# The modulation column loads of a two-block network move from SyncE's DMA queue to GpSimd's

## What is computed

```
# block 1
mod = silu(c) @ w_ada + b_ada                    # shift, scale, gate: 3 x 2048
h   = rms_norm(x) * (1 + scale) + shift
z   = h @ w_in                                   # u, v, g, q, k, v, g, f (f has 16 columns)
y   = concat(spatial gating, forgetting attention) @ w_out
x   = x + gate * y
# block 2: layer 0 (context + gated linear attention + conv), layer 1 (pooling mixer)
mod_i = silu(c_2) @ w_ada_2[i] + b_ada_2[i]      # 3 x 2048 for each of two layers
modc  = silu(c_ctx_2) @ w_ada_2[0]               # shift and scale of the 256 context tokens
x   = layer_norm(alpha * x + gate_i * mixer_i(x * (1 + scale_i) + shift_i))
```

## Time and profile before

| | |
|---|---|
| runs, median of 3 | 3305.11 us (3304.21 to 3306.54) |
| span of the profiled execution | 3300.8 us |
| its own time, taken as the median | 3305.11 us, so 4.3 us lie around the span |
| PE busy (matmul) | 2958.6 us, 90% |
| PE weight load | 2348.7 us, 71% |
| DVE busy | 1836.1 us, 56% |
| ACT busy | 1066.8 us, 32% |
| POOL busy | 3.9 us, 10 instructions |
| DMA | 451.54 MB, mean 137 GB/s, 41.4% of 16 engines |
| PE in the chain that ended last | 80% |
| mean granted TensorE clock | 0.942 |

### The profile page before, as it was taken

The page is one execution under the profiler, slowest core; times in us unless marked ns, Lnnn a source line. Parts: engine busy times, 40 slices in busy tenths (PEclk is TensorE's granted clock), DMA queues, the critical chain, the costliest instruction groups (busy, mean ns, idle before and its releaser), DMA issues.

```text
span 3300.8 us, 39727 instructions
## 1 busy us (share of the span) xinstructions
PE 2958.6 (90%) x13275; PEld 2348.7 (71%) x13275; DVE 1836.1 (56%) x2889; ACT 1066.8 (32%) x1714; POOL 3.9 (0%) x10
## 2 busy tenths in 40 slices
PE   3499999989999969599999999999899698999996
PEld 2377887666777847378878687787788477787784
DVE  6857763444577454355437456473866666324443
ACT  2332222333332254322233435342322421223324
POOL 0000000000000000000000000000000000000000
PEclk8699999999999979799999999999999799999997
DMA  9766552222356436165522222224566263332331
GB/s 370 272 197 189 185 165 68 64 64 64 108 166 208 166 101 216 62 216 191 167 83 77 70 65 94 70 76 138 181 204 205 75 218 121 91 100 89 111 114 51
DMA packets 219344, 451.54 MB, mean 137 GB/s; under 512 B 23752, under 2 KB 29338, under 8 KB 214860
## 3 DMA queue, kind: packets, MB, share of 16 engines
q1 hardware_dynamic: 219212, 449.82, 41.4%
HBM read 422.47 MB, written 27.30 MB: 136 GB/s over the span
## 4 chain that ended last, share of the span: by engine, by line
PE 80%; DVE 6%; ACT 4%; issue 3%; DVEq 2%; DMA 2%; ACTq 1%; SPq 1%; PEldq 0%; PEld 0%
PE ps L1006 19%; PE ps L1008 19%; PE ps L1007 19%; PE ps L1015 3%; PE ps L1016 3%; PE ps L1017 3%; PE ps L1348 3%; PE ps L985 1%; PE ps L1058 1%; PE ps L1213 1%; PE ps L1221 1%; DMA a_raw<-in_w_ada 1%; DVE acc L1593 1%; PE ps L1381 1%; PE ps L1378 1%
## 5 line engine op out<-in xcount | busy, mean ns | idle before, releaser
L1006 PE MATMUL ps<-op_hi,w_hi 128*128 128x512 f32 (+2 forms) x2928 | 1186.0, 405 | 105.8 <-DVE op_lo L1505 47.3
L1008 PE MATMUL ps<-op_hi,w_lo 128*128 128x512 f32 (+2 forms) x2928 | 1158.4, 396 | 0.0
L1007 PE MATMUL ps<-op_lo,w_hi 128*128 128x512 f32 (+2 forms) x2928 | 1158.0, 396 | 0.0
L1006 PEld LDWEIGHTS ps<-op_hi,w_hi 128*128 128x128 f32 (+1 forms) x2928 | 562.9, 192 | 251.5 <-issue 58.3
L1457 DVE TENSOR_TENSOR w_lo<-w_raw,w_hi 128x512 fp32r<-128x512 f32 x496 | 342.3, 692 | 596.9 <-ACT w_hi L570 592.2
L1008 PEld LDWEIGHTS ps<-op_hi,w_lo 128*128 128x128 f32 (+1 forms) x2928 | 561.8, 192 | 122.5
L1007 PEld LDWEIGHTS ps<-op_lo,w_hi 128*128 128x128 f32 (+1 forms) x2928 | 563.8, 193 | 112.8 <-issue 1.7
L570 ACT ACTIVATE w_hi<-w_raw 128x512 fp32r<-128x512 f32 x496 | 313.0, 632 | 1022.1 <-PE ps L1008 849.1
L1419 DVE SCALAR_TENSOR_TENSOR acc<-a_raw,vec,acc 128x512 f32<-128x512 f32 x576 | 419.7, 747 | 22.5 <-DMA a_raw<-in_w_ada 22.0
L1405 DVE TENSOR_TENSOR w_lo<-w_raw,w_hi 128x512 fp32r<-128x512 f32 (+2 forms) x240 | 145.6, 610 | 207.7 <-ACT w_hi L546 206.8
L546 ACT ACTIVATE w_hi<-w_raw 128x512 fp32r<-128x512 f32 (+2 forms) x240 | 134.8, 565 | 366.8 <-PE ps L1008 285.6
(11 more groups left out here) (208 smaller groups left out, 2245.0 us busy)
## 6 DMA issues: line engine op xcount, KB each, us to landing
a_raw<-in_w_ada SPq DMA_DIRECT2D x224, 512.0 KB, 4.0
w_raw<-in_w_in_e SPq DMA_DIRECT2D x160, 512.0 KB, 4.3
w_raw<-in_w_in SPq DMA_DIRECT2D x112, 512.0 KB, 4.8
arena<-in_w_ada SPq DMA_DIRECT2D x64, 512.0 KB, 8.0
w_raw<-in_w_in_o SPq DMA_DIRECT2D x64, 512.0 KB, 4.2
w_raw<-in_w_out SPq DMA_DIRECT2D x32, 512.0 KB, 5.0
w_raw<-in_w_out_e SPq DMA_DIRECT2D x32, 512.0 KB, 5.0
w_raw<-in_w_out_o SPq DMA_DIRECT2D x32, 512.0 KB, 3.6
```

The lines of the kernel that those rows point to most:

```text
L1006: mm(dst, hi[:, cols], B.op_hi[:, k, 0:tok], start=first, stop=False)
L1007: mm(dst, hi[:, cols], B.op_lo[:, k, 0:tok], start=False, stop=False)
L1008: last = mm(dst, lo[:, cols], B.op_hi[:, k, 0:tok], start=False, stop=last_t)
```

## The change

The 224 loads of `a_raw` are taken out of SP's program and written into GpSimd's (`part_loads`), each with the wait that it had. SP's groups with a part become the same two-turn loop as the others. GpSimd's six memsets stand between the loads in program order.

```diff
-    def modulation(n, m):
-        part, o = GROUPS[n]["part"], ordinal(n)
-        if part is None:
-            return
-        ...
-        if o or m >= 2:
-            sp.wait_ge(sem("part_tile"), KT * o + 2 * m - 2)
-        sp.dma_start(B.a_raw[:, m % 2, :, :], src[:, 2 * m:2 * m + 2, c:c + GC]).then_inc(B.a_in[m % 2], 16)
-
     def stream(n, middle=None):
         pairs = GROUPS[n]["kt"] // 2
-        before = n and GROUPS[n - 1]["part"] is not None
-        if GROUPS[n]["part"] is None and not before and not middle and pairs == 8 and GROUPS[n]["name"] != "egb":
+        if n and not middle and pairs == 8 and GROUPS[n]["name"] != "egb":
             with sp.Fori(0, 2) as r:
                 for m in range(4):
                     weights(n, m, r)
@@
-            if m < LAG and before and not (middle and m == 2):
-                modulation(n - 1, 8 - LAG + m)
             if middle and m == 1:
-                if before:
-                    modulation(n - 1, 7)
                 middle()
-            if m >= LAG:
-                modulation(n, m - LAG)
@@
+def part_loads(B, pool, groups):
+    for n in groups:
+        part, o = GROUPS[n]["part"], ordinal(n)
+        if part is None:
+            continue
+        src = B.A["w_ada"][0] if part < 12 else B.A["w_ada_2"][(part - 12) // 12]
+        src = src.rearrange("(k p) n -> p k n", p=P)
+        c = part % 12 * GC
+        for m in range(KT // 2):
+            if o or m >= 2:
+                pool.wait_ge(B.sem("part_tile"), KT * o + 2 * m - 2)
+            B.nc.gpsimd.dma_start(B.a_raw[:, m % 2, :, :], src[:, 2 * m:2 * m + 2, c:c + GC]).then_inc(B.a_in[m % 2], 16)
+
 def pool_program(B, pool):
     nc, sem, at = B.nc, B.sem, B.at
     n = FIRST["wo1"]
+    pool.wait_ge(sem("masks_made"), 1)
+    part_loads(B, pool, range(FIRST["wo1"] + 1))
 
     pool.wait_ge(B.bank_free[n % 2], n // 2 + 1)
     nc.gpsimd.memset(at(AT_WGC, 1, 2048)[0:33, 0, :], 0.0)
@@
+    part_loads(B, pool, range(FIRST["wo1"] + 1, FIRST["r"]))
     pool.wait_ge(sem("states_out"), 1)
     nc.gpsimd.memset(at(AT_WG, 1, 512)[0:33, 0, :], 0.0)
@@
+    part_loads(B, pool, range(FIRST["r"], FIRST["beside"]))
+    pool.wait_ge(sem("beside_stored"), 16 * (2 * GLA_HEADS + 1))
+    part_loads(B, pool, range(FIRST["beside"], len(GROUPS)))
```

More of the change, by code:

```diff
@@ L300, in weights @@
                      B.weight(g)[:, tiles, g["col"]:g["col"] + g["width"]]).then_inc(B.w_in[slot], 16)
-    def modulation(n, m):
-        part, o = GROUPS[n]["part"], ordinal(n)
-        if part is None:
-            return
-        src = A["w_ada"][0] if part < 12 else A["w_ada_2"][(part - 12) // 12]
-        src = src.rearrange("(k p) n -> p k n", p=P)
-        c = part % 12 * GC
-        if o or m >= 2:
-            sp.wait_ge(sem("part_tile"), KT * o + 2 * m - 2)
-        sp.dma_start(B.a_raw[:, m % 2, :, :], src[:, 2 * m:2 * m + 2, c:c + GC]).then_inc(B.a_in[m % 2], 16)
     def stream(n, middle=None):
         pairs = GROUPS[n]["kt"] // 2
-        before = n and GROUPS[n - 1]["part"] is not None
-        if GROUPS[n]["part"] is None and not before and not middle and pairs == 8 and GROUPS[n]["name"] != "egb":
+        if n and not middle and pairs == 8 and GROUPS[n]["name"] != "egb":
             with sp.Fori(0, 2) as r:
```

## The result

The changed kernel takes 3325.43 us (median of 4 runs, 3323.34 to 3326.93) against 3304.66 us (3302.37 to 3306.54) of the kernel before on the same chip: ratio 1.0062, 95% interval 1.0048 to 1.0076. It is slower by 20.8 us. The prediction was slower, 3318.5 us, range 3306 to 3337.

A forecast was written before the change was run, and what follows sets the result against it. PE was taken to bound most of the chain, with late column loads setting DVE's pace in narrow groups. Terms 6.0 + 5.1 + 1.2 + 1.1 = 13.4 us raised the median 3305.1 to 3318.5 us, range 3306 to 3337.

The forecast's parts named there:

- The bound: PE makes 80% of the chain; it also passes through eight column loads, whose two-buffer loop holds DVE in narrow groups.
- e: Extra time from buffer free to column load landed when GpSimd issues it: 1.4 us, bounded between 0 and 4.
- "f": Group with four column loads on the chain, each later by 1.5 us: 6.0 us lost.
- "ck": Group with three column loads on the chain, each later by 1.7 us: 5.1 us lost.
- "r": Group where each two pairs go over their slack by 0.3 us, four times: 1.2 us lost; first load counted 0.
- "wo1" (1): Group whose first load now stands behind GpSimd's memsets, so PE gets a tile late: 1.1 us lost.
- The other groups: Groups with 12 matmuls a tile: about 7.4 us from release to next reader against 5.4 needed, so nothing added.
- SP's gain: SP is freed of 224 issues of 0.37 us and 1099.5 us of standing, hidden behind the weights' lead: 0.
- The signs: If right: DVE's a_raw wait 35 to 50 us, "f" pieces some 5.7 us, ACT's w_raw wait below 10 us.
- B: Rival: the new queue is nearly as quick as SP, e below 0.7; 3309.3 us at 0.4; chance 0.25.
- C: Rival: faster, column loads on their own ring land in 3.6 us; 3296.7 us; chance 0.09.
- D: Rival: DVE slowed while GpSimd writes its lists, 14 us more in "r"; 3333 us; chance 0.06.

The follow-up runs named there:

- single_by_sync: The kernel before, all loads by SP, with a_raw as four buffers of one k-tile and 448 loads of 256 KB: 3301.66 us, ratio 0.9990.
- sync_weights_first: The kernel before, all loads by SP, with LAG 4 instead of 3, so column loads stand right behind the weights: 3308.66 us, ratio 1.0012.
- wo1_loads_first: The changed kernel with GpSimd's three memsets behind the first two column loads of the second wo1 group, not ahead: 3318.12 us, ratio 1.0044.
- single_tiles: The changed kernel with a_raw as four buffers of one k-tile and 448 loads of 256 KB instead of 224 of 512 KB: 3305.93 us, ratio 1.0005.
- start_held: The changed kernel with GpSimd's first column load waiting until the first four pairs of weights have landed: 3320.89 us, ratio 1.0051.
- three_mended: The changed kernel with wo1 memsets behind two loads, GpSimd's first load held, and columns of f, ck and r by SP: 3306.84 us, ratio 1.0004.
- narrow_by_sync: The changed kernel with the column loads of f, ck and r (24 of 224) issued by SP as before: 3312.01 us, ratio 1.0023.
- single_mended: The changed kernel with 448 one-k-tile loads in four buffers, wo1 memsets moved behind two pairs, GpSimd's first load held: 3304.96 us, ratio 0.9999.

## Why the prediction was right, point by point

**The bound.** Right: the column loads on the chain. PE waits where I had said. That the loop of two buffers cost the kernel before something as well is suggested by single_by_sync (3.0 us by the medians), at the edge of the measurement.

**The size of e.** 1.4 us, 1.5 in "f" and 1.7 in "ck" with the order's share, against 1.29 measured with the order in it: about the right number, by luck, from wrong parts. I had put it on an issue as long as a memset of 1.81 us; the issue takes 0.72 us. I had given the order 0.1 to 0.3 us; it makes 0.64, half of e (sync_weights_first). I had left out the 0.42 us between free and issue. So the reason I gave for the value was only partly the true one, and its errors cancelled. The Trainium skill, "DMA: Bandwidth & Descriptors", section "Latency and other measured facts", has GpSimd's loads start 0.4 us after SP's. The 0.3 us between issue and landing (4.96 against 4.66) are near it; the first packets in the trace put it higher, 1.0 us after the start of SP's issue and 1.8 us after the start of GpSimd's (medians; 1.4 us at the least). My "e would be 0.4" from that page left out the two other parts.

**"f"**, 6.0 us: measured 3.9. The chain has three loads there and not four; once it passes through PE and ACT. Three times the measured e is 3.9, and the third, fifth and seventh load of the group, which go through the same buffer, are 1.1, 1.4 and 1.5 us longer from free to landed. I had multiplied by the four pieces of the earlier trace rows, as if the chain kept its form, and added 0.1 to each. **"ck"**, 5.1: measured 4.3. **"r"**, 1.2: measured 2.4, of which 1.1 are waits, the size that I had, and 1.3 the clock in the first matmuls of "ek". Of its eight loads six are used within 0.3 us of landing, where it was three before; its first load takes 7.87 us where it took 7.96.

**"wo1" (1)**, 1.1 us: measured 5.4. The first wait cost 0.7 us. The step that failed is "Its two steps (1.3 us) and the next `low_tile` (0.7 us) end at about 1036.0, and PE wants that tile at 1034.97": I stopped at the first wait (and had its two steps as 1.3 us, which are 1.41 in the earlier trace rows). Behind it came 2.0 us at `take_part` and 2.7 us of clock. That the whole hangs on the late first load together with the slow loads is shown by wo1_loads_first (0.0 lost) and by single_tiles (0.0 lost with the memsets in place).

**Not in the prediction: the clock.** The sum prices waits alone. Some 6.5 us of the lag, in "wo1" (2), in "ek", over the attention and ahead of "ck", are matmuls at the lower of the two levels, and about 1 us of it is given back behind "ek". Without them the lag would be some 16 us, an estimate from the rows above, against the sum of 13.4.

**Not in the prediction: the start.** The first two column loads no longer stand behind the first four weight loads. 1.7 to 2.1 us by the lag; start_held gives 1.7 us back at the first matmul and 1.1 at "f".

**The other groups, 0.** Right for "q" to "v" (0.1 us) and nearly so for the groups from "ek" on (1.0 us in all, 2.0 of idle time less 1.0 of busy time); three_mended shows it with 200 loads on GpSimd.

**SP's gain, 0.** Right: its standing moved to L299, and the waits of ACT for `w_raw` are 14.3 us in all, 13.9 before. The sign of below 10 us failed; I had only the line of the earlier trace rows in mind.

**The attention and "gb", 1.9 us.** Not predicted. Five kernels lose 1.7 to 2.4 us there, the others nothing or less. In all five PE's busy time grows by 1.8 to 3.0 us and its idle time not at all, in the others the busy time grows by 0.5 us at most. So the loss is the granted clock's. Around two of PE's pauses there it stays 3.4 us longer at the lower level (625.6 to 639.2 and 792.8 to 806.5 in the changed kernel, 621.0 to 631.2 and 788.2 to 798.5 before). Why it does so in these five stays open: all have their columns from GpSimd, but so have narrow_by_sync, single_tiles and single_mended, which lose at most 0.2, and three_mended, which loses 2.4, begins the attention at the same time as the kernel before.

**The signs.** DVE's wait of 35 to 50 us became 70.1: the waits at group starts, which I priced at nothing, stand in it and cost little. The pieces in "f" grew to 4.6 to 5.5 us, not to 5.7. The wait at part tile 0 of "wo1" (1) is 5.43 us (predicted some 5), that of PE 0.56 us (about 1).

**The rivals.** B (as quick as SP) fell: e is 1.29. It was nearest for the half that is GpSimd's own, 0.65 us. C (faster on its own ring): none of its loads landed in 3.6 us, and single_mended, with a queue of its own and no other fault, is at 0.9999. D (DVE slowed) fell: 747 and 692 ns, unchanged. The Trainium skill's rule in "SBUF — State Buffer", section "SBUF: two separate sides", found nothing to act on, as its section "Who interferes with whom" has it for a subtraction like L1461.

My sum of 13.4 us stands against a lag of 21.6 us in the profile, 8.2 us short: "wo1" (1) 4.3, the start 1.7, the attention 1.9, "r" 1.2, the way to "ck" 0.9, all groups behind "ek" 1.0, "q" to "v" 0.1, less 2.1 in "f" and 0.8 in "ck". The range held because the places and about the size of e were right and the upper end allowed for an e of 2.9, not because the sum was; that the loss is half as large again as forecast comes from "wo1" (1) and the clock, which no term of it had. (Its lower end, 3306, is not what its formula gives at an e of 0.1; that is 3307.)

## What to carry to other kernels

Before a load moves to another queue, ask from buffer free to landed and not from issue to landed, and ask what it passes on the engines: here the new place behind the weights made half of the longer way, and one load that came to stand behind a 1 MB read took 10.0 us. A loop of two buffers that sets an engine's pace multiplies each tenth; cut into four half buffers of the same bytes, it took back nearly the whole loss on GpSimd, and on SP it was 3 us faster than the kernel before, at the edge of the measurement. A late load at a group's start must be followed to the group's end: with slow loads the lead does not return, and the bill comes at the next wait of the engine that matters. And a small loss is read twice, once as PE's idle time and once as its busy time for the same matmuls: nearly a third of this one was clock and no wait.

## What the runs showed of the hardware

A `drain` on GpSimd also waits for the DMAs that GpSimd has issued: of 222 loads none was issued sooner than 0.58 us after the landing of the one before (the median too is 0.58 us), and 1.00 us with two drains. Whoever puts memsets with drains between loads on that queue has one load in flight.

A 512 KB load on SP's queue with no other load in flight lands in 3.6 us (median of 136 weight loads of the kernel before, 3.4 to 5.4). Six weight loads of the attention stretch, three of them with a read of 256 KB in flight beside them:

```profile
L369 SPq DMA_DIRECT2D w_raw<-in_w_in x6: 372/373/373, 571.7 to 618.5; - x6
...
DMA to landing us min/median/max: 3.6/3.6/3.9
```

The size counts, and a line of weights does not show it by itself. The weight loads from 206 to 222 us are those of "f", of 112 KB. In the kernel before each has a column load 0.4 us ahead of it, in the changed kernel it goes first; the issues of that stretch, before and after:

```profile
a_raw<-in_w_ada SPq DMA_DIRECT2D x3, 512.0 KB, 3.8
w_raw<-in_w_in SPq DMA_DIRECT2D x3, 112.0 KB, 3.7
```

```profile
a_raw<-in_w_ada POOLq DMA_DIRECT2D x3, 512.0 KB, 4.1
w_raw<-in_w_in SPq DMA_DIRECT2D x3, 112.0 KB, 2.1
```

So a 112 KB load waits for the 512 KB load ahead of it, and the column load beside it takes 3.8 us, hardly more than alone. After the change the two do not share the engines here. From 207.7 to 210.0 only SP's queue (q1) moves bytes, from 210.0 to 212.5 only GpSimd's (q0); queue, packets, MB, share:

```profile
q1 hardware_dynamic: 272, 0.11, 22.0%
```

```profile
q0 software_dynamic: 144, 0.52, 75.7%
```

The column load of 208.64 that these packets belong to lands after 4.1 us. So a GpSimd load of 512 KB that shares with nothing takes 0.5 us more from issue to landing than SP's 3.6 us.
